# Splitting a weight tile with one 128x2048 instruction per engine in place of two of 128x1024

## The reference

```python
for l in range(2):                        # first_block
    h = rms_norm(x, attn_norm[l]); proj = h @ w_in[l]
    x = x + concat(mla(...), diff(...), chunk_band(...)) @ w_o[l]
    h = rms_norm(x, mlp_norm[l])
    x = x + square(relu(h @ w_up[l])) @ w_down[l]
x = rms_norm(x, final_norm)
h = concat(meta_tokens, x)                # second_block, once
    proj = rms_norm(h) @ w_in             # q, k, v, u
    attn = sliding_window_attention(q, k, v); ssm = s5_mixer(u)
    h = h + concat(rms_norm(attn), rms_norm(ssm)) @ w_out
    h = h + square(relu(rms_norm(h) @ w_up)) @ w_down
```

## Time and profile before

| what | us |
| --- | --- |
| median of 3 runs | 3577.96 |
| lowest, highest | 3568.64, 3578.29 |
| span of the profiled execution | 3574.1 |
| busy in it: PE matmul, PE weight load | 3356.0, 3211.0 |
| busy in it: DVE, ACT, POOL | 1942.7, 1425.8, 815.4 |

### The profile page before, as it was taken

The page is one execution under the profiler, slowest core; times in us unless marked ns, Lnnn a source line. Parts: engine busy times, 40 slices in busy tenths (PEclk is TensorE's granted clock), DMA queues, the critical chain, the costliest instruction groups (busy, mean ns, idle before and its releaser), DMA issues.

```text
span 3574.1 us, 67738 instructions
## 1 busy us (share of the span) xinstructions
PE 3356.0 (94%) x26098; PEld 3211.0 (90%) x26098; DVE 1942.7 (54%) x2525; ACT 1425.8 (40%) x2092; POOL 815.4 (23%) x876
## 2 busy tenths in 40 slices
PE   5999999999999998999999999887777999999999
PEld 4977999999999996899999999875546999999999
DVE  4545544544446544554444445699956544544444
ACT  3334433434335334433333334444334443434333
POOL 2100130303032200122121213257732230303030
PEclk9997999999999998899999999987768999999999
DMA  4550444555444453244445544421102444555444
GB/s 162 188 188 24 165 178 177 185 188 188 177 180 183 175 188 118 94 165 181 177 182 188 188 181 178 185 94 71 48 24 95 164 177 178 185 188 188 176 181 159
DMA packets 40240, 563.96 MB, mean 158 GB/s; under 512 B 4480, under 2 KB 4608, under 8 KB 6112
## 3 DMA queue, kind: packets, MB, share of 16 engines
q1 hardware_dynamic: 39024, 557.49, 42.7%
q10 hardware_dynamic: 720, 2.88, 0.2%
q0 software_dynamic: 416, 2.58, 0.2%
HBM read 560.84 MB, written 2.10 MB: 158 GB/s over the span
## 4 chain that ended last, share of the span: by engine, by line
PE 81%; DVE 8%; issue 6%; ACT 2%; POOL 2%; DMA 0%; ACTq 0%; DVEq 0%; POOLq 0%; SPq 0%
PE bank L531 81%; DVE w_lo L1189 2%; DVE mprod L1453 1%; DVE mprod L1459 1%; DVE zr L1466 1%; DVE ph L1437 1%; DVE zi L1467 1%; DVE ph L1432 0%; DMA raw<-stream 0%; PE bank L646 0%; POOL ssb L1687 0%; POOL cssb L1731 0%; ACT prob L964 0%; DVE nsum L1532 0%; PE bank L775 0%
## 5 line engine op out<-in xcount | busy, mean ns | idle before, releaser
L845 ACT ACTIVATE w_hi<-raw 128x1024 fp32r<-128x1024 f32 x1032 | 1036.0, 1052 | 1686.8 <-PE bank L531 1686.8
L1189 DVE TENSOR_TENSOR w_lo<-raw,w_hi 128x1024 fp32r<-128x1024 f32 x1032 | 1239.4, 1242 | 333.0 <-ACT w_hi L845 332.4
L531 PE MATMUL bank<-xg_hi,w_hi 128*128 128x256 f32 (+1 forms) x4352 | 1240.0, 285 | 93.3 <-DVE w_lo L1189 56.0
L531 PE MATMUL bank<-xg_lo,w_hi 128*128 128x256 f32 (+1 forms) x4352 | 1240.2, 285 | 0.0
L531 PE MATMUL bank<-xg_hi,w_lo 128*128 128x256 f32 (+1 forms) x4352 | 1239.1, 285 | 0.0
L531 PE MATMUL bank<-act_hi,w_hi 128*128 128x256 f32 x3904 | 1109.6, 284 | 21.4 <-DVE act_lo L1545 19.5
L531 PE MATMUL bank<-act_lo,w_hi 128*128 128x256 f32 x3904 | 1107.0, 284 | 0.0
L531 PE MATMUL bank<-act_hi,w_lo 128*128 128x256 f32 x3904 | 1106.8, 284 | 0.0
L531 PEld LDWEIGHTS bank<-xg_hi,w_hi 128*128 128x128 f32 x4352 | 837.0, 192 | 111.2 <-DVE w_lo L1189 49.6
L531 PEld LDWEIGHTS bank<-xg_hi,w_lo 128*128 128x128 f32 x4352 | 838.2, 193 | 0.0
L531 PEld LDWEIGHTS bank<-xg_lo,w_hi 128*128 128x128 f32 x4352 | 831.9, 191 | 0.0
(11 more groups left out here) (264 smaller groups left out, 1857.6 us busy)
## 6 DMA issues: line engine op xcount, KB each, us to landing
raw<-stream SPq DMA_DIRECT2D x264, 2048.0 KB, 7.7
x<-xT ACTq DMA_DIRECT2D x4, 512.0 KB, 8.7
out<-x SPq DMA_DIRECT2D x4, 512.0 KB, 6.5
cbias_sb<-cbias SPq DMA_DIRECT2D x2, 768.0 KB, 9.1
bm<-bmat POOLq DMA_DIRECT2D x1, 1024.0 KB, 5.4
cm<-cmat POOLq DMA_DIRECT2D x1, 1024.0 KB, 7.3
tab<-tables ACTq DMA_DIRECT2D x1, 768.0 KB, 13.4
tab<-tables POOLq DMA_DIRECT2D x1, 344.0 KB, 3.3
```

Of the source, the lines that this page charges most:

```text
L531: return pe.matmul(o, a, b, start=start, stop=stop, skip_group_check=True)
L845: act.activation(hi[j][:, 8 * h:8 * h + 8, :], raw[r][:, 8 * h:8 * h + 8, P * j:P * j + P], ACT.Copy)\
L1189: dve.tensor_tensor(lo[j][:, 8 * h:8 * h + 8, :], raw[r][:, 8 * h:8 * h + 8, P * j:P * j + P], hi[j][:, 8 * h:8 * h + 8, :].bitcast(F32), ...
```

## The change

Each split becomes one instruction per engine over the whole 128x2048 tile. DVE's part waits for the whole `hi`, and PE waits for the whole `lo` before its first matmul of the tile. Semaphores count one per tile in place of two, also in SP's wait ahead of a load. Nothing else moves.

```diff
-        def lo_count(T, half):
-            return 2 * T + half + 9
+        def lo_count(T):
+            return T + 5
...
-                sp.wait_ge(lo_ready, 4 * R + 12)
+                sp.wait_ge(lo_ready, 2 * R + 6)
...
                 pe.wait_ge(evac_done, T + 1)
-                for h in range(2):
-                    pe.wait_ge(lo_ready, lo_count(T, h))
-                    for k in range(8 * h, 8 * h + 8):
-                        if before is not None:
-                            before(k)
-                        last = row_tile(b, j, rhs_hi, rhs_lo, k)
+                pe.wait_ge(lo_ready, lo_count(T))
+                for k in range(KT):
+                    if before is not None:
+                        before(k)
+                    last = row_tile(b, j, rhs_hi, rhs_lo, k)
...
-                    if k % 8 == 0:
-                        pe.wait_ge(lo_ready, lo_count(T, k // 8))
+                    if k == 0:
+                        pe.wait_ge(lo_ready, lo_count(T))
...
-                for h in range(2):
-                    act.activation(hi[j][:, 8 * h:8 * h + 8, :], raw[r][:, 8 * h:8 * h + 8, P * j:P * j + P], ACT.Copy)\
-                        .then_inc(hi_ready, 1)
+                act.activation(hi[j][:], raw[r][:, :, P * j:P * j + P], ACT.Copy).then_inc(hi_ready, 1)
...
-            dve.sem_inc(lo_ready, 8)
+            dve.sem_inc(lo_ready, 4)
...
-                for h in range(2):
-                    dve.wait_ge(hi_ready, 2 * T + h + 1)
-                    dve.tensor_tensor(lo[j][:, 8 * h:8 * h + 8, :], raw[r][:, 8 * h:8 * h + 8, P * j:P * j + P],
-                                      hi[j][:, 8 * h:8 * h + 8, :].bitcast(F32), ALU.subtract).then_inc(lo_ready, 1)
+                dve.wait_ge(hi_ready, T + 1)
+                dve.tensor_tensor(lo[j][:], raw[r][:, :, P * j:P * j + P], hi[j][:].bitcast(F32), ALU.subtract).then_inc(lo_ready, 1)
```

More of the change, by code:

```diff
@@ L799, in gate_half @@
                         pe.wait_ge(evac_done, evacuated(T - 2))
-                    pe.wait_ge(lo_ready, lo_count(T, 1))
+                    pe.wait_ge(lo_ready, lo_count(T))
                 o = bank[2 + t % 2][:, 256 * e:256 * e + 256]
```

## The result

| | before | after |
| --- | --- | --- |
| median, us | 3573.37 | 3595.45 |
| lowest, highest, us | 3568.64, 3578.29 | 3591.64, 3603.02 |
| span of the profiled execution, us | 3574.1 | 3600.9 |

The ratio after to before is 1.0065, with a 95% interval of 1.0045 to 1.0085: slower by 22 us. The medians are those of four runs of each, taken together. The profiled execution of after is its longest (3603.02 us), 7.6 us above the median, so its span is above a usual one too.

The account below looks back on a forecast made before the run. PE, multiplying during 94% of the span, was taken as the bound on average, DVE in the scan. Terms 9.4 + 9.25 + 1.7 + 3.7 + 1.4 + 0.8 - 6.0 = +20.2 us on 3577.96 gave 3598, range 3586 to 3607.

Parts of the forecast that it names:

- Kind 1, w = 1.07: Where PE already stands waiting for lo's first half, it now waits for the whole: 2.29 us after DVE's start, not 1.22.
- Kind 2, d = 0.78: DVE's split ends 0.78 us later, so POOL's work waiting behind it ends that much later too.
- d + w of 1.85: At a norm, POOL's last sum comes 0.78 us later and the first split behind it costs PE 1.07 more.
- Norms and attention: Five of six norms +9.25 us, inner norms of layers one and two +3.7, DVE's first attention scores +1.4.
- the 0.8 ahead of the scan: Ahead of the scan, high then low parts run with nobody covering, so the later split counts once: +0.8 us.
- The first norm, +1.7: Norm at the start: DVE's own sum 0.6 us later, plus PE's wait for the whole lo; bounds 1.1 to 2.1.
- Rounds: PE at k=12 of each round's first down tile waits 0.78 us longer for act_lo; 12 places, +9.4 us.
- I take a gain of 0.5 for each of 12 splits: -6.0: In the scan, bound by DVE, whole splits leave POOL no gap; bounds 0.07 to 0.86 us a split.
- the scan gives nothing back: Rival: in the scan POOL's turn only moves; +25.4 us, time 3603, chance 0.13.
- The first third-layer tiles ... I take 0: Where POOL works on 128x1024: lost head start against one POOL turn fewer, taken as 0; bounds -2 to +1 us.
- The clock at the inner norms: Rival: the granted clock falls in PE's longer waits at the inner norms, 3 us each; time 3604, chance 0.08.

Follow-up runs that it names:

- experiment 1: The kernel before, but PE waits for both halves of lo before a tile's first matmul; ACT and DVE keep their halves. Ratio 1.0020.
- Experiments 2 and 3: Two variants of the kernel before: first, ACT's piece whole and DVE's in halves, ratio 1.0015; second, DVE's piece whole and ACT's in halves, ratio 1.0069.
- Experiment 4: The kernel after, but in a round's first down tile PE waits for each act_lo singly from k=12 on. Ratio 1.0035 to before.
- Experiment 6: The kernel before, with whole splits only in the third layer's first eight tiles (2 to 9). A single run, 3581.24 us.
- experiment 7: ACT's squares ahead of the split, several kernels. Before's halves: all 0.9984, no up tiles 0.9972, output projections alone 0.9965. After's whole pieces: all 1.0052, up tiles alone 1.0060.

## Why the prediction was right, and where it wasn't

The forecast was 3598, the median is 3595.45, and 20.2 us were forecast for a measured 22. The mechanism was right; three terms of the sum were not, and that the total came so close owes something to luck, as the sum at the end of this section shows.

- **Kind 1, w = 1.07**: right. Shown by experiment 1, which has nothing else in it.
- **Kind 2, d = 0.78**: right in size, in the rounds (6.61 against 5.83 us) and in the norms: output projection and norm from the first add to PE's restart grew by 1.81 and 1.68 us for a forecast d + w of 1.85. But the prediction saw only that a later DVE makes POOL later. Experiments 2 and 3 say it better: a later start in halves gives POOL a turn at the seam; the price is that the long piece has no seam.
- **Norms and attention**: the waits of PE at the norms of the MLPs, 8.7, 8.7 and 8.6 us, are 10.4, 10.2 and 10.6, and the one ahead of the third layer went from 8.6 to 10.8. PE's wait at both inner norms went from 1.04 to 2.89 us, the forecast 1.85 to the digit. PE's wait for the scores of attention grew from 5.07 to 5.78 us in both layers, as forecast, and the 0.8 ahead of the scan came as 0.79 (from ACT's last split to the first product, 8.19 to 8.98 us).
- **The first norm, +1.7**: too large. PE restarts behind layer one's inner norm at 111.60 and not 109.29, 2.31 later, of which 1.85 are the inner norm's; 0.46 are left. Yet w is in it in full: PE restarts 2.34 us after DVE's split begins (58.14 to 60.48), and 1.27 before (58.78 to 60.05). DVE's last sum ends 0.41 later, for a forecast of 0.6. What took it back is POOL's reduction, which starts sooner behind POOL's step ahead of it. Timelines of POOL, before and after:

```profile
54.16 1.81 POOL L1687 PARTITION_ALL_REDUCE ssb<-ssum  x1 [8.50 <-issue]
```
```profile
53.53 1.81 POOL L1682 PARTITION_ALL_REDUCE ssb<-ssum  x1 [7.46 <-issue]
```

  That idle time differs by 1.04 us. In the profiles of all kernels here it lies between 7.0 and 8.5 us at this place, with halves (7.2 to 8.5) as with whole pieces (7.0 to 8.2), so that the term came out small looks like scatter and not like the change. No run tells what sets it.
- **Rounds**: right. From DVE's first add of one round's down tiles to that of the next it takes 183.91 us (533.20 to 717.11) and 183.12 before (533.79 to 716.91). The whole MLP of layer one grew by 3.06 us (644.70 against 641.64), close to 4 x 0.78, but that is chance: it also has w in it, and the half clock behind the restart lasted 6.0 us before and 3.4 in after. Experiment 4 takes the rounds' part out.
- **"I take a gain of 0.5 for each of 12 splits: -6.0"**: the term that failed. Each split did get shorter by 0.64, but the stretch lost 1.1 us. POOL's turn is owed, not avoided: what it doesn't get inside the split it takes at the next DVE instruction. That was the lower bound of the term (0.8 in all) and the rival "the scan gives nothing back", at 0.13; it is what happened. Where an engine is the bound, one counts its whole stretch, not the instruction that changes.
- **"The first third-layer tiles ... I take 0"**: also failed. The stretch grew from 39.77 to 41.75 us, outside the bounds' upper end of 1. PE's wait for one tile went from 0.73 to 2.68 us. Experiment 6 has 2.1 by itself once the clock is taken out, and in experiment 1 this stretch has PE's largest new wait: it is kind 1 again. The row of before in experiment 6 has the sign of it: PE stood there already, waiting for the first half.
- **The clock at the inner norms**: given 0.08, and it came in the profiled execution at one of two. Windows of after behind the waits of 2.89 us at the inner norms of layers one and two (the last three numbers are granted clock, DMA share and GB/s):

```profile
111.60:117.00 5.40, 5.40 (x45) 5.40 (x46) 5.40 (x6) 0.00 (x0) 3.38 (x4) 1.00 0.37 85
1244.64:1250.00 5.36, 5.36 (x25) 5.36 (x26) 5.36 (x6) 0.00 (x0) 3.47 (x4) 0.50 0.34 79
```

The second has 25 matmuls where the first has 45. It also came at a norm for which the prediction had no such rival, ahead of layer two. Windows of before and of after there, behind waits of 2.95 and 4.70 us:

```profile
1190.09:1195.00 4.91, 4.91 (x41) 4.91 (x42) 3.68 (x4) 0.26 (x1) 0.00 (x0) 1.00 0.13 27
```
```profile
1193.40:1199.40 6.00, 6.00 (x28) 6.00 (x29) 2.48 (x2) 0.00 (x0) 0.00 (x0) 0.50 0.40 106
```

From 1.00 to 0.50 is the step from 2.4 to 1.2 GHz. Each costs some 2.6 us: from the restart ahead of layer two to that at its inner norm it takes 51.24 us and not 46.71, of which 1.85 are the inner norm's. But in the same execution the clock also gave 4.9 us back, in the stretch behind the attention of layer one that experiment 1 shows for before (29.01 us at 0.53):

```profile
306.70:330.85 24.15, 21.61 (x80) 15.36 (x80) 18.27 (x45) 9.92 (x34) 0.00 (x0) 0.72 0.01 1
```

In layer two that stretch is the same in both kernels (27.90 and 27.89 us). The two falls and this gain nearly cancel, so the clock explains little of the 26.8 us between the two spans. How often each happens in the runs without a profile isn't known.

With the three terms as measured the sum would be 20.2 + 4.9 + 2.0 - 1.2 = 25.9 us. The two spans say 26.8. The medians say 22, and the interval of the ratio leaves 16 to 30. So the sum with the terms as measured fits both, and that the forecast of 20.2 lies so near to 22 is in part luck: it had the scan's gain too large by 4.9.

The Trainium skill (SBUF — State Buffer, "SBUF: two separate sides") says that the side that lacks the shared ports is blocked for the whole of the other's instruction. The rows agree in every kernel: 0.6 us from the end of DVE's piece to the end of `act_lo`, and 0.74 us for `act_lo` with no DVE piece beside it.

What stays open: of the 4.0 us that an output projection and its norm gain in experiment 7, 1.4 are POOL's earlier sum (from DVE's last add to its end it takes 2.48 us and not 3.93). The rest lies between that sum and the reduction over partitions, where the profile shows POOL waiting for nothing (9.39 us idle before, 5.81 then). No run tells what it does there; it is the same idle time that shortened the first norm.

## What to carry to other kernels

Before two instructions are merged to save their fixed cost, ask who uses the seam: a consumer that starts on the first half, and another engine that is locked out meanwhile. Here merging saved 0.07 us a tile on an engine with time to spare and took 22 us where there was no cover. A turn that another engine takes from the bound engine isn't saved by closing the gap it used; measure the stretch. And handing work to the blocked engine before the long instruction pays only while the ring that this closes stays shorter than the bound engine's tile: 5.76 us here, kept in the output projections and missed in the last down tiles. Nor does it pay behind a norm, where the handed-over work itself needs the norm's result and holds back the copy for which PE waits.

## What the runs showed that was not expected

- Two 128x1024 subtractions with POOL waiting take 2.91 us, and `act_lo` ends sooner (3.76 us after the tile's end) than when DVE starts 0.9 us earlier (4.05). A piece that starts later can let the other engine finish sooner.
- Waits of the same length, 2.89 us, left the granted clock at 1.00 at one inner norm and at 0.50 at the other in the same execution.
